# Memory key/value projection: token tiles stationary, weight panels of 512 outputs moving

## The reference, cut to what matters

```python
def rmsnorm(x, g):
    xf = x.astype(jnp.float32)
    y = xf * lax.rsqrt(jnp.mean(xf * xf, axis=-1, keepdims=True) + EPS)
    return (y * g.astype(jnp.float32)).astype(x.dtype)

def mem_kv(mem, g_mem, w_mem_kv, k_norm_mem):        # mem (1, 256, 1024), w_mem_kv (1024, 1024)
    B, M, _ = mem.shape
    kv = rmsnorm(mem, g_mem) @ w_mem_kv
    k = rmsnorm(kv[..., :MEM_WIDTH].reshape(B, M, MEM_HEADS, MEM_HEAD_DIM), k_norm_mem)   # 4 heads of 128
    v = kv[..., MEM_WIDTH:].reshape(B, M, MEM_HEADS, MEM_HEAD_DIM)
    return k, v
```

## Time and profile before

| | |
|---|---|
| median of 3 runs | 1262.4 us |
| the profiled execution | 1264.13 us, span 1262.1 us |
| TensorE matmul busy | 1223.3 us, 97% |
| VectorE, ScalarE, POOL busy | 985.2 us (78%), 664.3 us (53%), 79.1 us (6%) |
| mean granted TensorE clock | 0.995 of full speed |
| the memory projection's groups | from 80.99 us (layer 0) and 631.7 us (layer 1) |

### The profile page before, as it was taken

The page is one execution under the profiler, slowest core; times in us unless marked ns, Lnnn a source line. Parts: engine busy times, 40 slices in busy tenths (PEclk is TensorE's granted clock), DMA queues, the critical chain, the costliest instruction groups (busy, mean ns, idle before and its releaser), DMA issues. The chain is left out here.

```text
span 1262.1 us, 23615 instructions
## 1 busy us (share of the span) xinstructions
PE 1223.3 (97%) x9204; PEld 1184.7 (94%) x9204; DVE 985.2 (78%) x1614; ACT 664.3 (53%) x1218; POOL 79.1 (6%) x108
## 2 busy tenths in 40 slices
PE   6999999999999999999989999999999999999996
PEld 6998999999999999999988986699999999999996
DVE  4765557999999999976754466556999999999972
ACT  6656434454554555555863467534455555455442
POOL 1000000001001001102000100000001100100102
PEclk8999999999999999999999999999999999999999
DMA  6244022215325433524443320023224523532522
GB/s 219 71 131 137 18 84 84 79 56 142 98 77 131 115 93 94 137 86 149 134 109 111 105 72 2 1 78 90 68 60 111 135 75 104 129 101 81 136 82 84
DMA packets 209141, 122.03 MB, mean 97 GB/s; under 512 B 6059, under 2 KB 205387, under 8 KB 209032
## 3 DMA queue, kind: packets, MB, share of 16 engines
q1 hardware_dynamic: 198088, 101.24, 27.5%
q0 software_dynamic: 10752, 19.23, 6.5%
q10 hardware_dynamic: 192, 0.06, 0.0%
HBM read 106.54 MB, written 6.90 MB: 90 GB/s over the span
## 5 line engine op out<-in xcount | busy, mean ns | idle before, releaser
L1041 ACT ACTIVATE WH<-RAW 128x1024 fp32r<-128x1024 f32 (+2 forms) x149 | 144.2, 967 | 149.8 <-PE ACCP L1722 136.8
L1059 ACT ACTIVATE EH<-SB 128x1024 fp32r<-128x1024 f32 (+1 forms) x116 | 112.6, 970 | 171.9 <-DVE SB L1367 91.4
L1342 DVE TENSOR_TENSOR WL<-RAW,WH 128x1024 fp32r<-128x1024 f32 (+2 forms) x149 | 166.3, 1116 | 42.3 <-ACT WH L1041 41.3
L1373 DVE TENSOR_TENSOR EL<-SB,EH 128x1024 fp32r<-128x1024 f32 (+1 forms) x116 | 128.7, 1109 | 5.0 <-ACT EH L1059 2.8
L1722 PE MATMUL ACCP<-XH,WH 128*128 128x288 f32 x512 | 112.5, 302 | 3.7 <-DVE XL L1476 3.7
L1722 PE MATMUL ACCP<-XL,WH 128*128 128x288 f32 x512 | 110.3, 297 | 0.0
L1722 PE MATMUL ACCP<-XH,WL 128*128 128x288 f32 x512 | 110.2, 297 | 0.0
L1732 PE MATMUL MISC<-BH,EH 128*128 128x288 f32 x360 | 106.8, 297 | 1.6 <-DVE EL L1373 1.5
L1732 PE MATMUL ACCP<-BH,EH 128*128 128x288 f32 x360 | 106.9, 297 | 0.0
L1732 PE MATMUL ACCP<-BL,EH 128*128 128x288 f32 x360 | 106.2, 295 | 0.0
L1732 PE MATMUL MISC<-BL,EH 128*128 128x288 f32 x360 | 106.2, 295 | 0.0
(11 more groups left out here) (320 smaller groups left out, 3545.2 us busy)
## 6 DMA issues: line engine op xcount, KB each, us to landing
RAW<-in_w_gu SPq DMA_DIRECT2D x88, 512.0 KB, 4.2
RAW<-in_w_down SPq DMA_DIRECT2D x48, 384.0 KB, 4.1
RAW<-in_w_in SPq DMA_DIRECT2D x16, 512.0 KB, 4.0
RAW<-in_w_mem_kv SPq DMA_DIRECT2D x16, 512.0 KB, 3.8
RAW<-in_w_out SPq DMA_DIRECT2D x16, 512.0 KB, 3.9
X<-PC POOLq DMA_DIRECT2D x48, 144.0 KB, 2.8
RAW<-in_w_down SPq DMA_DIRECT2D x16, 256.0 KB, 2.9
RAW<-in_w_kv SPq DMA_DIRECT2D x8, 512.0 KB, 3.6
```

Source lines behind the costliest of these rows:

```text
L1041: a.activation(WH[:, w % SPLIT_SLOTS, 0:nk, 0:ncol], RAW[:, p % RAW_SLOTS, 0:nk, 0:ncol], ACT.Copy).then_inc(split_ready(w, True)[0], 1)
L1059: a.activation(EH[:, first:first + n, 0:nh], mixtures(s)[:, first:first + n, 0:nh], ACT.Copy).then_inc(block_hi, n)
L1342: v.tensor_tensor(WL[:, w % SPLIT_SLOTS, 0:nk, 0:ncol], RAW[:, p % RAW_SLOTS, 0:nk, 0:ncol], WH[:, w % SPLIT_SLOTS, 0:nk, 0:ncol], ALU.sub ...
L1373: v.tensor_tensor(EL[:, first:first + n, 0:nh], mixtures(s)[:, first:first + n, 0:nh], EH[:, first:first + n, 0:nh], ALU.subtract).then_in ...
```

## The change

The operands change roles, in both layers. The stationary tile is now 128 tokens of one input chunk (MH or ML), and the moving one is a weight panel 512 outputs wide and two input chunks deep, again 512 KB and 8 panels. Two sums over the eight chunks (e = 0: keys, e = 1: values), four panels each, end token-major in PSUM, one bank per 128 tokens. So:

- A wide panel is rounded in two instructions of 512 elements per engine, one for each input chunk, and TensorE may begin with the first chunk when its two parts are there.
- Tokens' inverse norms (TR) come from ScalarE alone, which squares MRAW with a sum along the row; the sums on TensorE and the additions on VectorE go.
- VectorE evicts two times 512 columns times TR into MKTOK or MV, once for each sum. The copies to MKTOK and MV and the transposes ahead of them go.
- Keys' norms: ScalarE squares MKTOK whole, VectorE sums by head, ScalarE makes KR, VectorE scales eight blocks in place, with the gain from a row GAIN that POOL loads spread over the partitions. Then eight transposes in one job turn MKTOK into MKT.

```diff
-        for c in range(2 * HC):
-            kind = "mk" if c < HC else "mv"
...
-                g = group(colsof(w_mem[layer], c * P, (c + 1) * P), P, "m", kind, c=c % HC,
-                          first=c == 0, xs=layer * KC, layer=layer)
...
+        for e in range(2):
+            g = take("acc")
+            for j in range(HK):
+                def make(e=e, j=j, g=g, layer=layer):
+                    add("mem_group", g=g, e=e, j=j, layer=layer, first=j == 0, last=j == HK - 1,
+                        **panel(lambda: w_mem[layer][:, 2 * j:2 * j + 2, e * W2:(e + 1) * W2], 2, W2))
+                step_group(now, make)
+                now += 1
+                spread(1)
+                if (e, j) == (0, HK - 1):
+                    add("key_squares", layer=layer, g=g)
+                elif (e, j) == (1, 0):
+                    add("key_norm", layer=layer)
+                elif (e, j) == (1, 2):
+                    turn("mkt", layer=layer)
...
                 elif s.kind == "store" and s.name == "mem":
-                    gp.wait_ge(misc_free, s.m)
+                    gp.wait_ge(keys_normed, MK * HC * (s.layer + 1))
+                    gp.wait_ge(acc_free, s.g + 1)
...
+                if p in wide_panels:
+                    a.activation(hi[:, 0], raw[:, 0], ACT.Copy).then_inc(first_hi, 1)
+                    a.activation(hi[:, 1], raw[:, 1], ACT.Copy).then_inc(hi_ready, 1)
+                    return
...
+                elif s.kind == "token_norm":
+                    act.wait_ge(mem_loaded, 16 * (s.layer + 1))
+                    for t in range(MK):
+                        if t or s.layer:
+                            act.wait_ge(token_squares, 3 * s.layer + t)
+                        a.activation(GU[:, 0:D], MRAW[:, t], ACT.Square, accum_out=TSS[:, t:t + 1]).then_inc(token_squares, 1)
...
+                elif s.kind == "key_squares":
+                    act.wait_ge(acc_free, s.g + 1)
+                    act.wait_ge(token_squares, 3 * s.layer + 3)
+                    a.activation(GU[:, 0:D], MKTOK.rearrange("p t n -> p (t n)"), ACT.Square).then_inc(keys_squared, 1)
...
+                if p in wide_panels:
...
+                    dve.wait_ge(first_hi, wide_panels.index(p) + 1)
+                    v.tensor_tensor(lo[:, 0], raw[:, 0], hi[:, 0], ALU.subtract).then_inc(first_lo, 1)
+                    dve.wait_ge(*split_ready(w, True))
+                    v.tensor_tensor(lo[:, 1], raw[:, 1], hi[:, 1], ALU.subtract).then_inc(lo_ready, 1)
+                    return
...
+                elif s.kind == "mem_group":
+                    if s.last:
+                        dve.wait_ge(panel_used, s.q + 1)
+                        dve.wait_ge(token_r, s.layer + 1)
+                        for t in range(MK):
+                            dst = MV if s.e else MKTOK
+                            v.tensor_scalar(dst[:, t], ACCP[:, s.g % 2, t], TR[:, t:t + 1], None,
+                                            ALU.mult).then_inc(acc_free if t == MK - 1 else half_taken, 1)
+                    split_lo(s.sn + 2)
...
+                elif s.kind == "key_norm":
+                    dve.wait_ge(keys_r, 2 * (s.layer + 1))
+                    dve.wait_ge(gain_loaded, 16 * (s.layer + 1))
+                    for n in range(MK * HC):
+                        key = MKTOK[:, n // HC, n % HC * P:(n % HC + 1) * P]
+                        v.scalar_tensor_tensor(key, key, KR[:, n:n + 1], GAIN[:], ALU.mult, ALU.mult).then_inc(keys_normed, 1)
...
+                elif s.kind == "mem_group":
+                    if s.first and s.g >= 2:
+                        pe.wait_ge(acc_free, s.g - 1)
+                    pe.wait_ge(first_lo, wide_panels.index(s.p) + 1)
...
+                    for k in range(2):
+                        kc = 2 * s.j + k
+                        if k:
+                            pe.wait_ge(lo_ready, s.q + 1)
+                        if s.e == 0:
+                            pe.wait_ge(ml_ready, KC * s.layer + kc + 1)
+                        for t_ in range(MK):
+                            cols = slice(t_ * P, (t_ + 1) * P)
+                            for e, (m, w) in enumerate(((MH, wh), (MH, wl), (ML, wh))):
+                                ins_ = t.matmul(ACCP[:, s.g % 2, t_], m[:, kc, cols], w[:, k], start=kc == 0 and e == 0,
+                                                stop=kc == KC - 1 and e == 2)
+                    ins_.then_inc(panel_used, 1)
...
-                elif s.kind == "rm":
-                    misc_ready(s.m)
-                    pe.wait_ge(ml_ready, KC * (s.r + 1))
-                    sums(s.m, ONES[:].bitcast(F32), TG, MT_TOK)
```

More of the change, by code:

```diff
@@ L410, in mem_split @@
         def mem_split(c):
-            return lambda: add("mem_split", layer=layer, c=c, s=take("msq"), jobs=marks["memt", layer])
+            return lambda: add("mem_split", layer=layer, c=c, jobs=marks["memt", layer])
         now = 0
@@ L447, in encoder_kernel @@
                 marks["memt", layer] = count["job"]
+                add("token_norm", layer=layer)
                 fill += [mem_split(c_) for c_ in range(KC)]
                 fill.append(lambda: add("load_caches", layer=layer, m=marks["memt", layer], mh=(layer + 1) * KC))
-                fill.append(lambda: add("rm", m=take("job"), r=take("rm")))
                 if layer == 1:
@@ L454, in encoder_kernel @@
                 spread(2 if layer == 0 else 3)
[L456 to L469 removed]
+        for e in range(2):
[13 more added lines that the diff above has]
+                    turn("mkt", layer=layer)
+        values_g = g
         if layer == 0:
@@ L477, in encoder_kernel @@
                 now += 1
-            store("mem", layer=layer, m=count["job"])
+            store("mem", layer=layer, g=values_g)
         else:
@@ L726, in moving_of, with panel_in @@
         def moving_of(kind):
-            return {"x": (XH, XL, xl_ready, T), "y": (HH, HL, yl_ready, T),
-                    "m": (MH, ML, ml_ready, MT_TOK)}[kind]
+            return {"x": (XH, XL, xl_ready, T), "y": (HH, HL, yl_ready, T)}[kind]
+        def panel_in(slots, slot, p):
+            nk, ncol = panel_shape[p]
+            if ncol <= P:
+                return slots[:, slot, 0:nk, 0:ncol]
+            return slots[:, slot].rearrange("p k n -> p (k n)").rearrange("p (k n) -> p k n", n=ncol)
         def split_ready(w, high):
@@ L817, in evac @@
             ps = ACCP[:, s.g % 2]
[L818 to L822, removed]
             dve.wait_ge(r_ready, 2 * s.layer + 1)
@@ L919, in _ @@
                         load(s.p, s.view)
-                elif s.kind in ("lead", "project"):
+                elif s.kind in ("lead", "project", "mem_group"):
                     load(s.p, s.view)
@@ L977, in _ @@
                     gp.wait_ge(ml_ready, s.mh)
+                    gp.wait_ge(token_squares, 3 * s.layer + 2)
                     gp.wait_ge(misc_done, s.m)
```

92 lines of the change are left out of this document (45 added, 47 removed).

## The result

The changed kernel takes 1251.41 us (median of 4 runs, 1250.37 to 1252.56), beside it the kernel before 1262.15 (4 runs, 1260.61 to 1263.42): ratio 0.9914 [0.9901, 0.9926], 10.7 us faster. Forecast: 1251.1, range 1247.5 to 1256.5.

What follows compares the result with a forecast made beforehand. TensorE, busy 97% of the span, was taken as the bound. Terms of 0.43, 0.35, 5.19, 4.71, 0.22 and 0.43 sum to 11.3 us: profiled 1264.1 becomes 1252.8, or 1251.1 for the median, 1.7 lower; range 1247.5 to 1256.5.

Steps and rivals of the forecast that it cites:

- tokens' sum, layer 0: Before layer 0's memory projection: the token sum of squares leaves TensorE, where it has no wait; gain 0.43 us.
- first two groups, layer 0: Layer 0's first two memory groups: two-part rounding lets VectorE's window sums start 0.4 earlier; gain 0.35 us.
- the other six and the tail: Layer 0, third memory group to first scores: 25.67 us becomes 20.48, with a tail of 3.4; gain 5.19.
- tokens' sum, layer 1: Stretch before layer 1's memory projection: the token sum of squares leaves TensorE, where it has no wait; gain 0.43 us.
- first two groups, layer 1: Layer 1's first two memory groups: TensorE already waits for ScalarE's chain behind them, so a shorter group waits longer; gain 0.
- the other six: Layer 1, third memory group to shared projection: 21.79 us becomes 17.08; gain 4.71.
- fourth value transposes, layer 1: Inside layer 1's shared K/V projection: the fourth pair of value transposes goes; gain 0.22 us.
- Rival A: Memory product: wide matmul takes 239 ns, saving nothing itself; +2.0 us, 1253.1; chance 0.14 shared with late VectorE.
- D: Memory product: 512-column matmuls run at the plain f32 rate, 0.93 us each; +135 us, 1386; chance 0.01.
- Rival E: Memory product: a wide matmul takes the skill's sustained 131 ns; 13.5 us more gained, 1237.6; chance 0.01.
- The cover of the keys: VectorE's key scalings end 7.0 us after the fourth group, TensorE's key transposes come at 8.1; cover 1.1 us.
- Rival C: Panel transfers become the limit: without overlap each group lasts a 3.8 us landing; 1264.3, slower than before; chance 0.02.

Runs made afterwards that it cites:

- values: Kernel before, with value groups evicted straight into MV feature-major, without the values' transposes and copies (attention reads wrong values): 1258.25 us, ratio 0.9965.
- keys: Kernel before, without the memory keys' norm and transposes, keys stored as they lie in MKT: 1253.93 us, ratio 0.9936.

## Why the prediction was right

Step by step, in stretches of the two profiles:

| term | predicted | measured |
|---|---|---|
| tokens' sum, layer 0 (HRAW to first memory matmul) | 0.43 | 0.43 (45.73 to 45.30) |
| first two groups, layer 0 | 0.35 | 0.38 (9.73 to 9.35) |
| the other six and the tail | 5.19 | 5.25 (25.67 to 20.42) |
| tokens' sum, layer 1 (scores to first memory matmul) | 0.43 | 0.09 (515.33 to 515.24) |
| first two groups, layer 1 | 0 | -0.08 |
| the other six | 4.71 | 4.56 (21.79 to 17.23) |
| fourth value transposes, layer 1 | 0.22 | not separable: 0.54 in a stretch that varies by 1.3 |
| sum | 11.3 | 10.6 and the last line |

- *The price of a 512-column matmul.* Taken 225 ns from bounds of 213 and 239, measured 227. Six groups are 72 matmuls, so 0.15 us less gained per layer than forecast, which is all of layer 1's miss (4.56 for 4.71). In layer 0 the same 0.15 is hidden by the tail, forecast 0.23 too long, so the 5.25 for 5.19 is in part luck. Rival A (239) falls, and so does D, the rate of the plain f32 products. Of the two figures of the Trainium skill ("TensorE: Matmul & The Clock Gate", Back-to-back issue gap) neither holds here: its rule would give 216 at 512 columns, its sustained figure is 131, and the trace has 227 with a weight load ahead of each. Rival E falls with it.
- *The first two groups.* The waits grew to 1.62 and 1.05 in layer 1 (forecast some 1.6 and 1.1), for they end with a chain on ScalarE and VectorE that doesn't care how fast TensorE is. The 0.08 lost in layer 1 is what rounding in two parts adds to that chain, 0.1 by the run that rounds whole; the prediction put it at 0.05 and left it out. Taking the chain away (norms a group later) gave 5.2 us; taking width away shortened the waits. Shown from both sides.
- *Layer 0's start.* The 0.35 for the two-part rounding was put down to VectorE's window sums starting earlier; rounding whole brings back 0.36 there. Shown.
- *The follow-up jobs.* 0.43 and 0.22 each and 1.3 for the wait in the middle: 3.88 per layer for the keys where 3.9 was expected. Shown. The tail of 3.4 came out at 3.17 (105.73 to 108.90). Its wait of 1.27 stands where 1.14 stood before; moving the jobs ahead of it brought nothing.
- *The cover of the keys.* 1.1 forecast, 0.9 found, and its loss priced at 2.0 per layer. The eight scalings took 2.18 us, 0.26 from start to start; the prediction had a little less.
- *The transfers.* Rival C had panels at 3.8 us a landing without overlap. Landings after are 3.7 us, and SyncE issues some panels much closer than that:

```profile
96.79 0.37 SPq L914 DMA_DIRECT2D RAW<-in_w_out  x1
99.14 0.37 SPq L914 DMA_DIRECT2D RAW<-in_w_out  x1
```

  Issues 2.35 us apart and landings of 3.7 overlap, and TensorE waited for no panel. But the need was softened by the panels loaded ahead: in the five groups of layer 0 DMA moved 150 GB/s, which is a panel per 3.5 us and not per 2.73. Whether one per 2.73 us could be kept up for long, no run shows.
- *The term that was mis-sized.* In the stretch from layer 0's scores to layer 1's first memory matmul 0.34 of the forecast 0.43 is missing. The tokens' sum is not at fault: from the norm that it stood behind to the end of the next group the kernel before takes 7.34 us (610.18 to 617.52) and the changed one 6.91 (602.88 to 609.79), 0.43 less. What failed is that the other work of the stretch was taken to keep its time. Two of layer 1's eight input groups ran faster in the kernel before than any of the last five does in the changed one. The first of the two, before and then changed, from its first matmul to the job behind it:

```profile
597.04 0.42 PE L1722 MATMUL ACCP<-XH,WH 128*128 128x288 f32 x2
...
603.28 0.29 PE L1842 MATMUL MISC<-SQH,BLK 128*128 128x288 f32 x1
```

```profile
589.58 0.43 PE L1761 MATMUL ACCP<-XH,WH 128*128 128x288 f32 x2
...
595.96 0.30 PE L1892 MATMUL MISC<-SQH,BLK 128*128 128x288 f32 x1
```

  That is 6.24 and 6.38 us for 48 matmuls, 130.0 and 132.9 ns each; the other group went from 6.24 (618.06 to 624.30) to 6.38 (610.32 to 616.70), and the prediction's 130.0 was read in it. Together they lose 0.28; the other 0.06 are differences of 0.01 to 0.03 along the way. The two kernels made from the one before have the fast groups too, all profiles of the changed kernel and its variants the slow ones, so this goes with the change; what makes them slower stays open.

  A wait in this stretch is marked in the changed kernel alone, but it is not the cause:

```profile
477.81 0.40 PE L1771 MATMUL ACCP<-HBH,EH 128*128 128x288 f32 x1 [0.17 <-DVE EL L1401]
```

  In the kernel before the same matmul comes late too, without a bracket:

```profile
484.93 0.29 PE L1732 MATMUL ACCP<-HBH,EL 128*128 128x288 f32 x1
485.27 0.40 PE L1732 MATMUL ACCP<-HBH,EH 128*128 128x288 f32 x1
```

  Here 0.34 lies between two starts that are 0.13 apart elsewhere, and from the scores to this matmul the two kernels take 368.88 and 368.91 us. In three runs (values, keys, rounding whole) the matmul comes 0.3 earlier, which is the 0.3 by which their stretches (515.03, 515.01, 514.92) are shorter than those of the kernels that they are made from. Why VectorE is earlier there stays open.

The forecast set the sum (11.3) against the profile's own time and then moved it to the median of runs. The profile itself fell by 12.6; 1.4 of that is the earlier start, which is taken as no part of the change because one kernel made from the one before starts at 33.47 as well. By the medians the gain is 10.7, by the stretches 10.6 and the last line of the table. By stretches 0.48 is missing: 0.34 between the layers, 0.15 for the price of the wide matmul in layer 1, 0.08 in layer 1's first two groups, less 0.09 gained in layer 0. That 1251.1 and 1251.4 lie only 0.3 apart is partly luck: the gain was 0.6 less, but the kernel before itself stands at 1262.15 in the result and stood at 1262.4 in the forecast.

## What to carry to other kernels

When one engine is busy 97% of the time, count the small jobs between its large ones and the waits beside them: here they made some 8 of the 10.7 us and the wider product 1.8. Before crediting a faster piece, look at the instruction behind it; if that one already waits for another engine's chain, the piece gives nothing until the wait is moved, and moving it (asking for the norms a group later) was worth 5.2 us, about half of what the whole change brought. A wait taken away is a gain only if the next link of its chain is not queued behind something else: compare the tail of layer 0, where 1.27 us went and 2.14 came.

## What the runs showed of the hardware

- A wait of TensorE costs 0.20 to 0.25 us more than the idle time in the trace: two waits of 1.81 lengthened their stretches by 2.01 each, and four waits of 4.50 in all, when they went, gave 5.48. Part of it, 0.08, is seen at the matmul behind a wait: the distance to the next one is 0.21 (628.68 to 628.89) where it is 0.13 without. Short waits stand in no bracket: 0.34 between two starts at 485.27 of the kernel before has none.
- fp32r matmuls with a weight load each: 119.6 ns at 256 columns, 130.0 or 132.9 at 288 (from group to group), 227 at 512, and 119.3 where two of 256 follow on one stationary tile. At 2.4 GHz, so 10 to 14 ns stand beside the columns at these three widths.
- The granted clock was 1.00 in all the stretches compared; only the first 30 us have less, with 0.75 to 0.89 from 10 to 20 us, and no edit decided how much.
